# Two sandwich-normed layers in one kernel: the up products of both ConvFFNs split into lower and upper 64 rows, with a bank for each half

## What is computed

```python
def conv_ffn(h, w_up, conv_w, conv_b, w_down):          # w_up: 1024 x 5632
    up = h @ w_up
    gate = causal_dwconv(up[..., :FFN_HIDDEN], conv_w, conv_b)   # FFN_HIDDEN = 2816, width 3
    val = up[..., FFN_HIDDEN:]
    return (jax.nn.silu(gate) * val) @ w_down

for i in range(DEPTH):                                   # DEPTH = 2
    h = rms_norm(x, mix_pre_g[i])
    m = ssd_mixer(h, ...) if i == 0 else shortconv_mixer(h, ...)
    x = x + rms_norm(m, mix_post_g[i])
    f = conv_ffn(rms_norm(x, ffn_pre_g[i]), ffn_w_up[i], ffn_conv_w[i], ffn_conv_b[i], ffn_w_down[i])
    x = x + rms_norm(f, ffn_post_g[i])
```

## Time and profile before

| | us |
|---|---|
| median of 3 runs (lowest 1344.51, highest 1344.74) | 1344.51 |
| the profiled execution | 1345.21 |
| its span, first to last instruction | 1343.5 |
| TensorE busy | 1332.1 (99%) |
| VectorE busy | 783.9 (58%) |
| ScalarE busy | 568.9 (42%) |
| mean granted clock of TensorE | 0.999 |

### The profile page before, as it was taken

The page is one execution under the profiler, slowest core; times in us unless marked ns, Lnnn a source line. Parts: engine busy times, 40 slices in busy tenths (PEclk is TensorE's granted clock), DMA queues, the critical chain, the costliest instruction groups (busy, mean ns, idle before and its releaser), DMA issues.

```text
span 1343.5 us, 15937 instructions
## 1 busy us (share of the span) xinstructions
PE 1332.1 (99%) x6474; PEld 1116.8 (83%) x6474; DVE 783.9 (58%) x1139; ACT 568.9 (42%) x875; POOL 24.8 (2%) x28
## 2 busy tenths in 40 slices
PE   8999999999999999999999999999999999999998
PEld 7888888888888988888888888888898888888886
DVE  4888888888525566656542265445566666654223
ACT  6666655566316434333331172222554433333112
POOL 0000000000000000000000000000000000000000
PEclk9999999999999999999999999999999999999999
DMA  4533233432331233333343313334223333333331
GB/s 144 168 101 100 86 107 111 125 111 79 108 121 55 79 96 109 99 104 96 95 125 113 101 54 94 94 98 132 70 69 105 110 94 96 102 101 126 96 108 63
DMA packets 181773, 135.70 MB, mean 101 GB/s; under 512 B 5645, under 2 KB 169893, under 8 KB 180677
## 3 DMA queue, kind: packets, MB, share of 16 engines
q1 hardware_dynamic: 181653, 134.62, 33.4%
q10 hardware_dynamic: 48, 0.07, 0.0%
HBM read 132.51 MB, written 2.16 MB: 100 GB/s over the span
## 4 chain that ended last, share of the span: by engine, by line
PE 98%; ACT 1%; DMA 0%; DVE 0%; SPq 0%; issue 0%; DVEq 0%; ACTq 0%
PE bank L850 22%; PE bank L852 22%; PE bank L851 22%; PE bank L913 9%; PE bank L911 9%; PE bank L912 9%; PE bank L1031 1%; PE bank L1039 1%; PE bank L888 1%; PE bank L1021 1%; PE bank L1014 1%; PE bank L1006 1%; DMA pages<-in_ssd_norm_w 0%; PE bank L1009 0%; ACT h_hi L370 0%
## 5 line engine op out<-in xcount | busy, mean ns | idle before, releaser
L850 PE MATMUL bank<-h_hi,w_hi 128*128 128x512 f32 (+1 forms) x1352 | 513.0, 379 | 0.0
L852 PE MATMUL bank<-h_lo,w_hi 128*128 128x512 f32 (+1 forms) x1352 | 510.9, 378 | 0.0
L851 PE MATMUL bank<-h_hi,w_lo 128*128 128x512 f32 (+1 forms) x1352 | 510.8, 378 | 0.0
L585 DVE TENSOR_TENSOR w_lo<-w_raw,w_hi 128x1024 fp32r<-128x1024 f32 x228 | 285.8, 1257 | 321.6 <-ACT w_hi L355 321.6
L355 ACT ACTIVATE w_hi<-w_raw 128x1024 fp32r<-128x1024 f32 x228 | 238.1, 1052 | 195.8 <-PE bank L913 172.1
L852 PEld LDWEIGHTS bank<-h_lo,w_hi 128*128 128x128 f32 x1352 | 254.3, 188 | 47.5
L851 PEld LDWEIGHTS bank<-h_hi,w_lo 128*128 128x128 f32 x1352 | 254.4, 188 | 46.6
L850 PEld LDWEIGHTS bank<-h_hi,w_hi 128*128 128x128 f32 x1352 | 254.4, 188 | 46.4
L911 PE MATMUL bank<-w_hi,hid_hi 128*128 128x512 f32 x416 | 162.4, 390 | 0.0
L913 PE MATMUL bank<-w_hi,hid_lo 128*128 128x512 f32 x416 | 161.9, 389 | 0.0
L912 PE MATMUL bank<-w_lo,hid_hi 128*128 128x512 f32 x416 | 161.8, 389 | 0.0
(11 more groups left out here) (146 smaller groups left out, 944.1 us busy)
## 6 DMA issues: line engine op xcount, KB each, us to landing
w_raw<-in_ffn_w_up SPq DMA_DIRECT2D x88, 512.0 KB, 3.8
w_raw<-in_ssd_w_in SPq DMA_DIRECT2D x48, 512.0 KB, 3.9
w_raw<-in_ffn_w_down SPq DMA_DIRECT2D x44, 512.0 KB, 3.6
w_raw<-in_sc_w_in SPq DMA_DIRECT2D x24, 512.0 KB, 3.7
acs_b<-acs_dram SPq DMA_DIRECT2D x8, 1024.0 KB, 6.4
w_raw<-in_ssd_w_out SPq DMA_DIRECT2D x16, 512.0 KB, 3.6
w_raw<-in_sc_w_out SPq DMA_DIRECT2D x8, 512.0 KB, 3.6
x_tok<-in_x SPq DMA_DIRECT2D x4, 512.0 KB, 5.3
```

Of the source, the lines that this page charges most:

```text
L585: nc.vector.tensor_tensor(w_lo[slot(u)][:], w_raw[:, u % 2, :], w_hi[slot(u)][:].bitcast(F32), ALU.subtract).then_inc(w_lo_done, 1)
L850: nc.tensor.matmul(dst, wh, xh, start=start, stop=False)
L851: nc.tensor.matmul(dst, wl, xh, start=False, stop=False)
L852: return nc.tensor.matmul(dst, wh, xl, start=False, stop=stop)
```

## The change

From the third tile of each FFN (unit 4 on, `WHOLE = 4`) a unit is written by `unit_by_rows` in place of `unit`. Each matmul of 128 rows becomes two of 64 rows, one over input features 0 to 63 of the block and one over 64 to 127, which go to the array's lower and upper rows; they alternate, and each half sums into a bank of its own. A unit thus has 48 matmuls and two banks, and eight banks take turns in four pairs (`UP_PAIRS`). VectorE has to add the two banks: `both_rows` copies the one bank into `side`, adds the other, and only then follows the multiplication by `r_row`, which now reads `side`. `both_rows` waits after each of its two operations. The waits for banks are adapted. 40 units in each FFN change, 2 x 40 x 24 = 1,920 matmuls into 3,840.

```diff
+    UP_PAIRS = [((2, 3), (4, 5), (6, 7), (0, 1)), ((4, 5), (6, 7), (0, 1), (2, 3))]
+    WHOLE = 4
...
+            def both_rows(dst, pair):
+                nc.vector.tensor_copy(dst[:], bank[pair[0]][:]).then_inc(half_copied, 1)
+                joined[0] += 1
+                dve.wait_ge(half_copied, joined[0])
+                nc.vector.tensor_tensor(dst[:], dst[:], bank[pair[1]][:], ALU.add).then_inc(both_joined, 1)
+                dve.wait_ge(both_joined, joined[0])
...
+                whole = 2 * t < WHOLE
                 dve.wait_ge(unit_done, u + 1)
-                nc.vector.tensor_tensor(cpad[:, CW - 1:CW - 1 + T], bank[banks[0]][:], r_row[:, 0, :], ALU.mult).then_inc(gate_in, 1)
+                if whole:
...
+                else:
+                    both_rows(side, pairs[0])
+                    nc.vector.tensor_tensor(cpad[:, CW - 1:CW - 1 + T], side[:], r_row[:, 0, :], ALU.mult).then_inc(gate_in, 1)
                 splits_to(u + 4)
                 taps(n, lambda tap: col_ffn_w(layer, tap, t))
                 dve.wait_ge(unit_done, u + 2)
-                nc.vector.tensor_tensor(side[:], bank[banks[1]][:], r_row[:, 0, :], ALU.mult).then_inc(side_in, 1)
+                if whole:
...
+                else:
+                    both_rows(side, pairs[1])
+                    nc.vector.tensor_tensor(side[:], side[:], r_row[:, 0, :], ALU.mult).then_inc(side_in, 1)
...
+            def unit_by_rows(u, lower, upper):
+                pe.wait_ge(w_lo_done, u + 1)
+                hi, lo = w_hi[slot(u)], w_lo[slot(u)]
+                halves = ((slice(0, HD), lower), (slice(HD, P), upper))
+                for k in range(KT):
+                    cols = slice(k * P, (k + 1) * P)
+                    for w, x, first, final in ((hi, h_hi, True, False), (lo, h_hi, False, False), (hi, h_lo, False, True)):
+                        for rows, dst in halves:
+                            last = nc.tensor.matmul(dst, w[rows, cols], x[rows, k, :], start=first and k == 0, stop=final and k == KT - 1)
+                last.then_inc(unit_done, 1)
...
-                for n in range(AHEAD, 2 * FT):
+                gates, sides = HID0[2 * layer], (0, FT + 2 * WT)[layer]
+                for n in range(AHEAD, WHOLE):
+                    unit(U_UP[layer] + n, bank[banks[n]][:])
+                for n in range(WHOLE, 2 * FT):
                     t = n // 2
-                    if t >= 2:
-                        if n % 2 == 0:
-                            pe.wait_ge(gate_in, HID0[2 * layer] + t - 1)
-                        else:
-                            pe.wait_ge(side_in, (0, FT + 2 * WT)[layer] + t - 1)
-                    unit(U_UP[layer] + n, bank[banks[n % 4]][:])
+                    if n < WHOLE + 2:
+                        pe.wait_ge(gate_in, gates + 1)
+                    elif n < WHOLE + 4:
+                        pe.wait_ge(gate_in, gates + n - WHOLE - 1)
+                        pe.wait_ge(side_in, sides + n - WHOLE - 1)
+                    elif n % 2 == 0:
+                        pe.wait_ge(gate_in, gates + t - 1)
+                    else:
+                        pe.wait_ge(side_in, sides + t - 1)
+                    lower, upper = UP_PAIRS[layer][n % 4]
+                    unit_by_rows(U_UP[layer] + n, bank[lower][:], bank[upper][:])
...
-            project(back[1], hid_hi, hid_lo, hid_landed(HID0[0]), {2: taken(FT - 1, FT - 1), 3: taken(FT, FT)})
+            project(back[1], hid_hi, hid_lo, hid_landed(HID0[0]), {0: taken(FT - 1, FT - 1), 2: taken(FT, FT - 1), 3: taken(FT, FT)})
```

More of the change, by code:

```diff
@@ L254, in build @@
         pre_root, pre_done, row_mm, row_done, row2_done = (sem(n) for n in ("pre_root", "pre_done", "row_mm", "row_done", "row2_done"))
+        half_copied, both_joined = sem("half_copied"), sem("both_joined")
         gate_in, side_in, acc_done, tap_done, act_done, gated_done, hid_hi_done, hid_lo_done = (
@@ L788, in _ @@
             sides = [0]
+            joined = [0]
+            def both_rows(dst, pair):
[4 more added lines that the diff above has]
+                dve.wait_ge(both_joined, joined[0])
             def ffn_up(layer, t):
@@ L792, in ffn_up @@
                 banks = [UP_BANKS[layer][2 * (t % 2) + half] for half in range(2)]
+                pairs = [UP_PAIRS[layer][2 * (t % 2) + half] for half in range(2)]
+                whole = 2 * t < WHOLE
                 dve.wait_ge(unit_done, u + 1)
-                nc.vector.tensor_tensor(cpad[:, CW - 1:CW - 1 + T], bank[banks[0]][:], r_row[:, 0, :], ALU.mult).then_inc(gate_in, 1)
+                if whole:
+                    nc.vector.tensor_tensor(cpad[:, CW - 1:CW - 1 + T], bank[banks[0]][:], r_row[:, 0, :], ALU.mult).then_inc(gate_in, 1)
+                else:
+                    both_rows(side, pairs[0])
+                    nc.vector.tensor_tensor(cpad[:, CW - 1:CW - 1 + T], side[:], r_row[:, 0, :], ALU.mult).then_inc(gate_in, 1)
                 splits_to(u + 4)
@@ L797, in ffn_up @@
                 dve.wait_ge(unit_done, u + 2)
-                nc.vector.tensor_tensor(side[:], bank[banks[1]][:], r_row[:, 0, :], ALU.mult).then_inc(side_in, 1)
+                if whole:
+                    nc.vector.tensor_tensor(side[:], bank[banks[1]][:], r_row[:, 0, :], ALU.mult).then_inc(side_in, 1)
+                else:
+                    both_rows(side, pairs[1])
+                    nc.vector.tensor_tensor(side[:], side[:], r_row[:, 0, :], ALU.mult).then_inc(side_in, 1)
                 sides[0] += 1
@@ L1114, in _ @@
             g2, s2 = HID0[2], FT + 2 * WT
-            project(back[3], hid_hi, hid_lo, hid_landed(HID0[2]), {2: taken(g2 + FT - 1, s2 + FT - 1), 3: taken(g2 + FT, s2 + FT)})
+            project(back[3], hid_hi, hid_lo, hid_landed(HID0[2]), {0: taken(g2 + FT - 1, s2 + FT - 1), 2: taken(g2 + FT, s2 + FT - 1), 3: taken(g2 + FT, s2 + FT)})
 _INS = ["x", "mix_pre_g", "mix_post_g", "ffn_pre_g", "ffn_post_g", "ssd_w_in", "ssd_conv_w", "ssd_conv_b", "ssd_dt_bias",
```

## The result

| | before | changed |
|---|---|---|
| median, us | 1344.62 (1344.51 to 1344.77, 4 runs) | 1392.80 (1390.79 to 1393.74, 4 runs) |
| span of the profiled execution | 1343.5 | 1391.4 |
| TensorE, VectorE busy | 1332.1, 783.9 | 1350.5, 885.8 |
| mean granted clock | 0.999 | 0.994 |

The ratio is 1.0355 (95% interval 1.0343 to 1.0368): 48.2 us slower, where 46.8 were forecast.

What follows compares the result with a forecast made beforehand. VectorE was to replace TensorE as the bound: 2 x 21.3 us of lateness plus 4.2 for the clock is 46.8 on 1345.2, making 1392.0, or 1391.3 us against the median. Range 1368 to 1416.

Steps and rivals of the forecast that it cites:

- The loop: VectorE's time per up-product tile: 9.97 us grows by 1.77 to 11.74, over TensorE's 10.88.
- the gate half: Copy and addition before the gate's multiplication on VectorE: nothing covers them, +1.45 us a tile.
- the side half: Copy and addition for the side on VectorE: mostly inside an existing wait for ScalarE, +0.32 us a tile.
- the price from the 128x128 rows: VectorE's 128x512 copy priced like a two-input operation, 0.68 us, since at 128x128 they take 291 and 292 ns.
- up to twice the plain rate for a copy that reads PSUM: Rival: VectorE's copy is fast, loop 11.09 us a tile, time 1366; chance 0.05.
- weights, not banks: TensorE waits for VectorE's w_lo, making each layer 21.3 us late; new waits on banks cost nothing.
- The standstill: TensorE waits 5.6 us before the second unit of each down product, from 691.3 to 696.9 in layer 0.
- the clock: After TensorE's wait before the down product, a 4.2 us stretch at half pace costs 2.1 us a layer, +4.2.
- a choice between two bounds: After TensorE's 5.6 us wait: either nothing, or the program start's slow 4.2 us again; the latter was taken.
- The pair: Two half matmuls on TensorE cost 0.205 to 0.247 us; 0.2267 taken, so no added cost.
- The rival with faster pairs: VectorE keeps up and TensorE's 1,920 pairs save 12 ns each, 22 us: 1322; chance 0.04.
- The estimate of 0.249 for a pair: From the skill's page, a second row tile on TensorE adds a tenth: 0.249 us a pair, the whole 1400.

Runs made afterwards that it cites:

- join_gate: Kernel before, but only the gate's bank is copied and added to itself from the third tile on (gate doubled); 1379.14 us, ratio 1.0255.
- join_side: Kernel before, but only the side's bank is copied and added to itself from the third tile on (side doubled); 1344.68 us, ratio 1.0000.
- joins_late: Kernel before with whole matmuls, but VectorE copies each bank and adds it to itself from the 13th tile on; 1363.76 us, ratio 1.0137.
- filled: Changed kernel, with 23 added 128 x 128 products on TensorE ahead of each down product's second unit; 1387.79 us, ratio 1.0319.
- halves_only: Changed kernel without VectorE's copies and additions; the upper 64 rows' product is computed but not used; 1346.58 us, ratio 1.0009.
- scalar_first: Changed kernel, but ScalarE writes w_hi of unit u + 3 before it waits for the gate; 1346.31 us, ratio 1.0009.
- joins_only: Kernel before with whole matmuls, but VectorE copies each bank and adds it to itself from the third tile on; 1392.39 us, ratio 1.0356.

## Why the prediction came out right

**The loop.** 11.74 us was worked out, 11.73 measured, from +1.45 for the gate half and +0.32 for the side half. join_gate shows 11.42, which is 9.97 + 1.45; join_side shows 10.28, which is 9.97 + 0.32 to 0.01 us, and that this half is hidden when alone. The copy takes 0.68 us, so the price from the 128x128 rows held. The Trainium skill's table (VectorE: DVE Perf Modes, the perf-mode tier table) gives up to twice the plain rate for a copy that reads PSUM; that is a bound, and this copy reached nothing of it.

**Where TensorE waits.** The path was the forecast one: weights, not banks. A tile costs what VectorE's loop costs, from the third tile on, because VectorE comes late out of the boundary; joins_late shows the other case, in which ten tiles begin with VectorE in time, and the same arithmetic gives 1364 for 1363.8.

**The standstill and the clock.** 5.6 us were forecast ahead of the second down unit, 5.2 measured (5.47 less a usual step). Layer 0 is 21.3 us late at that matmul once the run's start, 0.34 us earlier than in the trace of before, is taken out. The term that was mis-sized is the clock: 2.1 us a layer, from a slow stretch of 4.2 us at the program's start, whereas the slow stretches in the trace last some 6.2 and 5.3 us. They cost 2.9 us in layer 0 and 2.5 in layer 1, compared with the same twenty steps in filled, and filled takes back 2.5 a layer. With 5.4 in place of 4.2 the sum is 1.2 us longer, and only 0.2 of the 1.4 us by which it was short remain. That a standstill would lower the clock at all was a choice between two bounds in the prediction, made from the nearer row. That row was read from the pace alone: the windows of before print a granted clock of 1.00 at the program's start too, but the trace has no record of the clock before 6.3 us. Here the granted clock itself shows the lower level.

**The pair.** 0.2267 was taken between 0.205 and 0.247, and is what halves_only shows. The rival with faster pairs had two conditions. scalar_first fulfilled the one, a loop of VectorE's under 10.3 us (10.88 less the 0.89 us of waiting for TensorE), and the pair's spacing stayed at 0.227. So 12 ns between the 0.215 of line 1021 and the 0.2267 here are not covered by the other half. What they are is open; no run here tried it. The estimate of 0.249 for a pair, from the four-tile figure in the Trainium skill (TensorE: Matmul & The Clock Gate, packing small matmuls), does not hold for this shape: in halves_only pairs are 0.227 apart.

**What was not tried.** One addition that reads both banks at once, in place of the copy and the addition, was not run.

## What to carry to other kernels

Room on an engine is not its idle share but the idle time that the bound engine ends; here 1.06 us of a tile of 10.88, against 42% idle on average. The same two operations cost nothing where they fall into a wait for a third engine and 34 us where that third engine waits behind them, so look first at the order on both engines; one moved line on ScalarE took back nearly the whole loss. And splitting the contraction over lower and upper rows did not speed up a product that already fills all 128 (512 columns, split float32): a pair takes 0.2268 us, one whole matmul 0.2267.

## What the runs showed of the hardware

- Two matmuls of 64 rows, one on the lower and one on the upper rows and in banks of their own, start 3 to 4 ns apart in steady state (halves_only, scalar_first). In the changed kernel, with its waits, they start 0.03 to 0.06 us apart. In both, each pair comes 0.227 us after the last, the step of one matmul of 128 rows.
- Unexpected: the two halves need not be neighbours in the program (one run each). At each change between them 3.3 matmuls of 512 columns overlap (0.73 to 0.76 us), so blocks of three are as good as strict alternation, and blocks of 12 or 24 lose 193 and 319 us.
- A standstill of 5.2 us was followed by 14 slow matmuls in layer 0 and 12 in layer 1 (join_gate: 10 and 8 after standstills of the same length), with a granted clock of 0.50, the level of 1.2 GHz; products without use in its place prevented that. What sets their number no run here shows. Idle steps of 0.7 to 0.8 us in every tile (joins_only, starts 0.997 apart) had no such consequence.
